# A two-block transformer layer in split float32: weight and feed-forward tiles placed 8 to 96 bytes further on in SBUF

## The chip, the cores and the metric

One core of a Trainium2 chip runs the kernel. The metric is the device time of one execution, in microseconds (us); smaller is better. A row names engines as PE (TensorE matmuls), PEld (TensorE weight loads), DVE (VectorE), ACT (ScalarE), POOL (GpSimd) and SP (SyncE, which issues the transfers).

## The reference, cut to what matters

A hybrid layer (pooling mixer, top-k attention, short convolution, feed-forward) is followed by a second layer (feed-forward, forgetting attention and stick-breaking attention, feed-forward, gated embedding). The model width is 1024, there are 512 tokens (528 with 16 meta tokens in the first layer), everything is float32. The change concerns only where the operands of the large products lie. Most of them come from the projections and from three feed-forward blocks of this form:

```
gate, up = jnp.split(hn @ w_gate_up, 2, axis=-1)      # 1024 x 5632
return h + (jax.nn.silu(gate) * up) @ w_down          # 2816 x 1024
...
x = x + 0.5 * swiglu(rms_norm_2(x, ffn1_norm), ffn1_w_gate, ffn1_w_up, ffn1_w_down)
...
x = x + 0.5 * swiglu(rms_norm_2(x, ffn2_norm), ffn2_w_gate, ffn2_w_up, ffn2_w_down)
```

## The kernel before, in words

Activations lie transposed in SBUF: features over the 128 partitions, tokens along a row. Every product is made of three matmuls, since each float32 operand is split in a high part in a reduced format (`F32R`) and a low part that is the rest: weights high times activation high (L608), weights high times activation low (L609), weights low times activation high (L610). In `passes` the weights are the stationary operand (loaded by a weight load, PEld) and the activations the moving one, mostly 512 columns of 4 bytes.

The weights come in 174 chunks of up to 2048 columns for each partition. A chunk c goes through two slots, c % 2: SP loads it into `raw[:, c % 2]`, ACT writes its high part into `whi[:, c % 2]` (L1079), POOL the low part into `wlo[:, c % 2]` (L500), PE uses both. A chunk of a square product is 8 row blocks k of 256 columns, so that PE's weight tiles start every 512 bytes in a slot. `chunk` walks t (2 output tiles) and k (8), three matmuls each; `pair` and the down projection in `ffn` do the same with other operands. The moving operands are `xh`/`xl` (the normalized activations, rows of 576 elements of which columns 16 to 527 are used by most chunks and all 528, in two halves of 264, by a few), the mixer and attention tiles in an arena, and in the down projection of each feed-forward block `fh`/`fl`, 22 rows of 512 elements. `fh` is written by ACT (L1123) and `fl` by DVE (L1584) while the gate and up projections run; PE reads both only in the down projection.

Placement: tiles are allocated one behind the other, rounded to 32 bytes, and `lead` pads the arena so that its start leaves 128 when divided by 256. Adding up the sizes gives that both slots of `whi` and `wlo`, column 16 of every row of `xh` and `xl`, and every row of `fh`, `fl` and of the other moving tiles of L608 to L610 leave the same 128. So in the products with 512 columns all operands have one phase modulo 256 bytes. Exceptions are the two halves of 264 columns (192 and 224 bytes from the weights' phase), the 8-column weights of chunk `C_FL` (a step of 32 bytes with each k), and in the stick-breaking attention `sk21`, the moving tile of L977 for odd heads, which starts 64 bytes before that phase; for even heads `sk20` has the common phase. L977 is followed there by L978, a 128-column matmul.

Of the kernel before, what the change touches and what calls it, by code (L numbers as in the profile page):

```python
# [20 lines left out]
F32 = mybir.dt.float32  # L21
F32R = mybir.dt.float32r
ACT = mybir.ActivationFunctionType
ALU = mybir.AluOpType
AX = mybir.AxisListType

P = 128
D = 1024
DK = D // P
T = 512  # L30
# [5 lines left out]
CH = 2048  # L36
# [9 lines left out]
FK = D_FF // P  # L46
HEAD_DIM = 64
DOWN_K = (8, 8, 6)
NEG = -1.0e30
UNITS = 4  # L50
Z_TOP = 60.0
TAKEN = -3.0e38
# [35 lines left out]
def lin(value, per=0, i=None):  # L88

    return value if i is None else i * per + value  # L90


def one(t, n):

    return t[:, n, :] if isinstance(n, int) else t[:, bass.ds(n, 1), :].rearrange("p o t -> p (o t)")
# [7 lines left out]
def build(nc, I, out):  # L103
    with ExitStack() as ctx:
        def sb(name, shape, dt=F32):
            return ctx.enter_context(nc.sbuf_tensor(name, shape, dt))
# [9 lines left out]
        eps = sb("eps", [P, 1])  # L116
        m8 = sb("m8", [P, 8])
        raw = sb("raw", [P, 2, CH])
        whi = sb("whi", [P, 2, CH], F32R)
        wlo = sb("wlo", [P, 2, CH], F32R)  # L120
        rs = sb("rs", [P, TM])
        rt = sb("rt", [P, TM])
        sq = sb("sq", [P, TM])
# [26 lines left out]
        def at(name, off, shape, dt=F32):  # L150
            n = 1
            for s in shape[1:]:
                n *= s
            assert off + n <= arena_cols, name
            return nc.alloc_sbuf_tensor_at(name, shape, dt, offset=start + 4 * off)


        fh = at("fh", 0, [P, FK, T], F32R)
        fl = at("fl", FK * T, [P, FK, T], F32R)
        tmp = at("tmp", 2 * FK * T, [P, 4, T])  # L160
        sq2, ssum2 = tmp[:, 0, :], tmp[:, 1, :]

        cT = at("cT", 0, [P, TM])
# [52 lines left out]
        rtq = at("rtq", 22528, [P, 4, T])  # L216
        pu = at("pu", 22528, [P, UNITS, T])
        sel = at("sel", 24576, [P, HEADS, P])
# [46 lines left out]
        silu_done, h_done, h_hi, h_split = sem("silu_done"), sem("h_done"), sem("h_hi"), sem("h_split")  # L265
# [215 lines left out]
        def _(pool):  # L481
# [6 lines left out]
            pool.affine_select(out=ident[:], in_=ident[:], compare_op=ALU.not_equal, fill=1.0, base=0, **tri).then_inc(consts, 1)  # L488
            pool.affine_select(out=causal[:], in_=causal[:], compare_op=ALU.is_ge, fill=NEG, base=0, **tri).then_inc(consts, 1)
            pool.affine_select(out=strict[:], in_=strict[:], compare_op=ALU.is_ge, fill=NEG, base=-1, **tri).then_inc(consts, 1)  # L490
            for z, o in enumerate((0, HEAD_DIM)):
# [113 lines left out]
        def _(pe):  # L605
# [74 lines left out]
            def ffn(f, S, X):  # L680
                c = C_F[f]

                chunk(c, xh, xl, X=X, between=lambda: norm_sums(S, c))
                chunk(c + 1, xh, xl)
                with pe.Fori(0, FK // 2 - 1) as i:
                    for j in range(2):
                        chunk(c + 2 + j, xh, xl, 2, i)
                c = C_D[f]
                with pe.Fori(0, 2) as i:
                    for j in range(2):  # L690
                        for r, kn in enumerate(DOWN_K):
                            cr, k0 = c + 3 * j + r, sum(DOWN_K[:r])
                            pe.wait_ge(w_lo, lin(cr + 1, 6, i))
                            if j == 0:
                                pe.wait_ge(h_split, FK * f + k0 + kn)
                            for t in range(2):
                                if r == 0:

                                    pe.wait_ge(acc_free, lin(2 * (c - 2 + j) + t + 1, 4 * j + 2 * t + 6, i))
                                for k in range(kn):  # L700
                                    o = CW * k + P * t
                                    mm = passes(ps[:, bank(c + j, t), :], cr % 2, lambda wt: wt[:, cr % 2, o:o + P],
                                                fh[:, k0 + k, :], fl[:, k0 + k, :], r == 0 and k == 0, r == 2 and k == kn - 1)
                                mm.then_inc(tile_done, 1)


# [350 lines left out]
            for n in range(DK):  # L1057
                if n >= 4:
                    pe.wait_ge(acc_free, 2 * C_PP + n - 3)
                for k in range(2):  # L1060
                    o = D * k + P * n
# [6 lines left out]
        def _(act):  # L1068
# [46 lines left out]
            def ffn(f, S, gain):  # L1115
                c = C_F[f]

                def up(c, n, per=0, i=None):
                    high(c + 2, per, i)
                    act.wait_ge(acc_free, lin(2 * c + 1, 2 * per, i))  # L1120
                    act.activation(tmp[:, 1, :], tmp[:, 0, :], ACT.Silu).then_inc(silu_done, 1)  # L1121
                    act.wait_ge(h_done, lin(FK * f + n + 1, per, i))
                    act.activation(one(fh, lin(n, per, i)), tmp[:, 3, :], ACT.Copy).then_inc(h_hi, 1)  # L1123

                root(S)
                if f == 1:
                    act.wait_ge(ms2_done, 1)
                    act.activation(rt[:, META:TM], ssum2, ACT.Sqrt, bias=eps[:], scale=1.0 / D).then_inc(rt2_done, 1)
                act.preload_act_table_set("silu_and_others")
                with act.Fori(0, FK // 2) as i:  # L1130
                    for j in range(2):
                        up(c + j, j, 2, i)
                d = C_D[f]
                with act.Fori(0, 2) as i:
                    for j in range(2):
                        high(d + 3 * j + 2, 6, i)
                        high(d + 3 * j + 3, 6, i)
                        act.wait_ge(acc_free, lin(2 * d + 6 * j + 3, 12, i))
                        feed(S + 1, 2 * j, gain, 4, i)
                        act.wait_ge(acc_free, lin(2 * d + 6 * j + 6, 12, i))  # L1140
                        feed(S + 1, 2 * j + 1, gain, 4, i)
                        high(d + 3 * j + 4, 6, i)
# [122 lines left out]
            for slot in range(4 * 2 * DK):  # L1265
                n = DSA_STEPS.get(slot)
# [225 lines left out]
        def _(dve):  # L1492
# [75 lines left out]
            def ffn(f, S, factor, gain):  # L1568
                c = C_F[f]
                if f == 1:  # L1570
                    closing_root()
                else:
                    root(S)
                with dve.Fori(0, FK // 2) as i:
                    for j in range(2):
                        n = FK * f + j
                        scaled(tmp[:, 0, :], c + j, 0, 2, i)
                        scaled(tmp[:, 2, :], c + j, 1, 2, i)
                        dve.wait_ge(silu_done, lin(n + 1, 2, i))
                        dve.wait_ge(acc_free, lin(2 * (c + j) + 2, 4, i))  # L1580
                        dve.tensor_tensor(tmp[:, 3, :], tmp[:, 1, :], tmp[:, 2, :], ALU.mult).then_inc(h_done, 1)  # L1581
                        dve.wait_ge(h_hi, lin(n + 1, 2, i))
                        nn = lin(j, 2, i)
                        dve.tensor_tensor(one(fl, nn), tmp[:, 3, :], one(fh, nn).bitcast(F32), ALU.subtract).then_inc(h_split, 1)  # L1584
                        dve.wait_ge(h_split, lin(n + 1, 2, i))
                d = C_D[f]
                if f == 1:
                    for n in range(DK):
                        x = hT[:, n, META:TM]
                        stt(x, x, vec[:, V_FIN + n:V_FIN + n + 1], ssum[:, META:TM], ALU.mult, ALU.mult).then_inc(xn_done, 1)  # L1590
                    dve.wait_ge(xn_done, DK)
                clear(S + 1)
                if S + 1 == 2:
                    dve.memset(ssum2, 0.0).then_inc(ssum2_done, 1)
                with dve.Fori(0, 2) as i:
                    for j in range(2):
                        for t in range(2):
                            n = 2 * j + t
                            done(d + 3 * j + 2, t, 6, i)
                            update(n, bank(d + j, t), factor, 3, 4, i)  # L1600
                            dve.wait_ge(acc_free, lin(2 * d + 6 * j + 3 * t + 3, 12, i))
                            feed(S + 1, n, gain, 4, i)
# [40 lines left out]
            for g in range(4):  # L1643
                r = slice(D_IDX * g, D_IDX * g + D_IDX)
# [25 lines left out]
            def search():  # L1670
                for q in range(QB):
# [4 lines left out]

                    link(stt(diag, causal[:], -TAKEN / -NEG, diag, ALU.mult, ALU.add))
                    for _ in range(TOP_K // 8):
# [3 lines left out]

                    link(dve.tensor_scalar(s, s, TAKEN, NEG, ALU.not_equal, ALU.mult))
                    link(dve.tensor_tensor(diag, diag, causal[:], ALU.add))
# [127 lines left out]
            for slot in range(4 * 2 * DK):  # L1812
                if slot % DK == DK - 1:
                    scaled(gb[:, slot // DK, :], C_GB + slot // (2 * DK), slot // DK % 2)
                n = DSA_STEPS.get(slot)
# [20 lines left out]
            with dve.Fori(0, 2) as i:  # L1836
                for n in range(4):
                    c, t = C_WB + n // 2, n % 2
# [66 lines left out]
            for z in range(2):  # L1905
                r = far(z).start + 32
# [119 lines left out]
            with dve.Fori(0, 2) as i:  # L2026
                for q in range(2):
                    c = C_MX + q
                    for t in range(2):
                        n = 2 * q + t  # L2030
# [62 lines left out]
```

## Time and profile before

| what | value |
|---|---|
| median of 3 runs | 2062.28 us (2061.86 to 2062.54) |
| profiled execution | 2061.71 us |
| its span in the trace | 2059.9 us |
| TensorE matmuls, busy | 2038.7 us, 9561 instructions |
| TensorE weight loads, busy | 1670.4 us |
| GpSimd / VectorE / ScalarE busy | 1009.8 / 883.7 / 734.4 us |
| DMA, mean | 91 GB/s |

A matmul's busy time overlaps that of its neighbours (a 512-column one is shown with 0.39 us, but a new one starts every 0.23 us), so the step from one start to the next is what counts, and it is read from a timeline. The granted clock of TensorE is 1.00, 2.4 GHz, in the stretches shown.

### The profile page before, as it was taken

The numbers are of one execution on the slowest core, as the hardware profiler recorded it, in microseconds if no ns is written. First come the engines' busy times: TensorE is split into PE (matmuls) and PEld (weight loads), VectorE is DVE, ScalarE is ACT, GpSimd is POOL, SyncE is SP. The second block draws the span as 40 slices with busy tenths as digits, with TensorE's granted clock in tenths as the row PEclk, the third lists the DMA queues.
The fourth block names the chain that finished last, engine by engine and source line by source line (L and its number), as shares of the span: only waits on it lengthen the run. The fifth ranks groups of instructions, "written<-read, shape, count | busy, mean of one in ns | idle before, by whom it ended". The sixth has DMA issues, their size and how long they took to land.

```text
span 2059.9 us, 26668 instructions
## 1 busy us (share of the span) xinstructions
PE 2038.7 (99%) x9561; PEld 1670.4 (81%) x9561; DVE 883.7 (43%) x1394; ACT 734.4 (36%) x1006; POOL 1009.8 (49%) x779
## 2 busy tenths in 40 slices
PE   8999999999999999999999999999999999999999
PEld 6798887678888888888888887888778888888887
DVE  6778645534333322153334113577744533332124
ACT  6413224433322223232222224566644422222232
POOL 5345442135555554455555444665544555554543
PEclk9999999999999999999999999999999999999999
DMA  4232322022333332333333232332222333333232
GB/s 159 66 103 83 103 89 74 21 79 85 102 102 100 85 96 93 99 100 102 98 86 97 92 98 82 107 99 72 70 64 82 102 102 98 86 101 97 92 107 82
DMA packets 254153, 188.21 MB, mean 91 GB/s; under 512 B 7552, under 2 KB 249728, under 8 KB 254080
## 3 DMA queue, kind: packets, MB, share of 16 engines
q1 hardware_dynamic: 253392, 186.93, 30.3%
q8 instruction: 44, 0.72, 0.1%
q10 hardware_dynamic: 688, 0.31, 0.1%
q14 instruction: 29, 0.24, 0.0%
HBM read 180.93 MB, written 2.10 MB: 89 GB/s over the span
## 4 chain that ended last, share of the span: by engine, by line
PE 95%; DVE 3%; issue 1%; ACT 1%; DMA 0%; SPq 0%; DVEq 0%; ACTq 0%
PE ps L608 29%; PE ps L610 29%; PE ps L609 29%; DVE sc L1502 1%; PE ps L988 1%; PE ps L829 1%; PE ps L895 1%; PE ps L814 1%; PE ps L897 1%; PE ps L896 1%; PE ps L960 0%; DVE ssum L1630 0%; PE ps L828 0%; PE ps L822 0%; PE ps L1002 0%
## 5 line engine op out<-in xcount | busy, mean ns | idle before, releaser
L500 POOL TENSOR_TENSOR wlo<-raw,whi 128x512 fp32r<-128x512 f32 (+1 forms) x640 | 870.6, 1391 | 923.3 <-ACT whi L1079 916.4
L608 PE MATMUL ps<-xh,whi 128*128 128x512 f32 (+2 forms) x1912 | 735.5, 385 | 9.3 <-DVE xl L1502 7.3
L610 PE MATMUL ps<-xh,wlo 128*128 128x512 f32 (+2 forms) x1912 | 722.1, 378 | 0.0
L609 PE MATMUL ps<-xl,whi 128*128 128x512 f32 (+2 forms) x1912 | 721.8, 378 | 0.0
L1079 ACT ACTIVATE whi<-raw 128x2048 fp32r<-128x2048 f32 (+1 forms) x159 | 297.6, 1871 | 797.8 <-PE ps L610 794.7
L608 PEld LDWEIGHTS ps<-xh,whi 128*128 128x128 f32 (+1 forms) x1912 | 357.9, 187 | 91.7 <-issue 23.9
L610 PEld LDWEIGHTS ps<-xh,wlo 128*128 128x128 f32 (+1 forms) x1912 | 357.7, 187 | 67.9
L609 PEld LDWEIGHTS ps<-xl,whi 128*128 128x128 f32 (+1 forms) x1912 | 358.3, 187 | 64.6 <-issue 2.5
L1556 DVE TENSOR_TENSOR tmp<-ps,rs 128x512 f32<-128x512 f32 x148 | 102.1, 691 | 325.9 <-PE ps L610 308.6
L608 PE MATMUL ps<-fh,whi 128*128 128x512 f32 x528 | 205.4, 389 | 0.0
L609 PE MATMUL ps<-fl,whi 128*128 128x512 f32 x528 | 205.4, 389 | 0.0
L610 PE MATMUL ps<-fh,wlo 128*128 128x512 f32 x528 | 205.4, 389 | 0.0
L1502 DVE SCALAR_TENSOR_TENSOR hT<-ps,hT 128x512 f32 x40 | 27.6, 691 | 271.0 <-PE ps L610 270.0
L1581 DVE TENSOR_TENSOR tmp<-tmp 128x512 f32<-128x512 f32 x66 | 90.2, 1367 | 114.3 <-ACT tmp L1121 114.2
L609 PEld LDWEIGHTS ps<-fl,whi 128*128 128x128 f32 x528 | 99.1, 188 | 20.6
L610 PEld LDWEIGHTS ps<-fh,wlo 128*128 128x128 f32 x528 | 99.1, 188 | 20.6
L608 PEld LDWEIGHTS ps<-fh,whi 128*128 128x128 f32 x528 | 99.1, 188 | 20.5
L555 POOL TENSOR_TENSOR wlo<-raw,whi 128x384 fp32r<-128x384 f32 (+1 forms) x78 | 77.1, 1016 | 42.8 <-ACT whi L1374 41.8
L1084 ACT ACTIVATE xh<-hT,vec (+1 forms) x48 | 34.4, 725 | 125.3 <-DVE hT L1502 125.3
L1123 ACT ACTIVATE fh<-tmp 128x512 f32 x66 | 41.8, 633 | 101.2 <-DVE tmp L1581 101.2
L1584 DVE TENSOR_TENSOR fl<-tmp,fh 128x512 f32 x66 | 51.0, 773 | 61.2 <-ACT fh L1123 61.2
L1502 DVE SCALAR_TENSOR_TENSOR xl<-hT,vec,xh (+1 forms) x48 | 47.0, 989 | 55.1 <-ACT xh L1084 55.1
(293 smaller groups left out, 2195.7 us busy)
## 6 DMA issues: line engine op xcount, KB each, us to landing
raw<-in_w_in SPq DMA_DIRECT2D x90, 512.0 KB, 4.6
raw<-in_w_gate_up SPq DMA_DIRECT2D x44, 512.0 KB, 4.7
raw<-in_ffn_w_gate SPq DMA_DIRECT2D x44, 512.0 KB, 3.9
raw<-in_ffn_w_up SPq DMA_DIRECT2D x44, 512.0 KB, 5.1
raw<-in_ffn_w_down SPq DMA_DIRECT2D x32, 512.0 KB, 4.0
raw<-in_w_down SPq DMA_DIRECT2D x16, 512.0 KB, 3.9
raw<-in_ffn_w_down SPq DMA_DIRECT2D x16, 384.0 KB, 3.5
raw<-in_w_b SPq DMA_DIRECT2D x8, 512.0 KB, 4.0
```

What stands on the lines that cost most here:

```text
L500: ins = pool.tensor_tensor(wlo[:, c % 2, cs], raw[:, c % 2, cs], whi[:, c % 2, cs].bitcast(F32), ALU.subtract)
L555: ins = pool.tensor_tensor(wlo[:, c % 2, cs], raw[:, c % 2, cs], whi[:, c % 2, cs].bitcast(F32), ALU.subtract)
L608: pe.matmul(o, w_of(whi), xhi, start=first, stop=False)
L609: pe.matmul(o, w_of(whi), xlo, start=False, stop=False)
L610: return pe.matmul(o, w_of(wlo), xhi, start=False, stop=last)
L1079: act.activation(whi[:, c % 2, 0:n], raw[:, c % 2, 0:n], ACT.Copy).then_inc(w_hi, 1)
L1084: act.activation(one(xh, nn)[:, lo:TM], one(hT, nn)[:, lo:TM], ACT.Copy, scale=col(vec, lin(gain + n, per, i))).then_inc(xh_done, 1)
L1123: act.activation(one(fh, lin(n, per, i)), tmp[:, 3, :], ACT.Copy).then_inc(h_hi, 1)
L1502: return dve.scalar_tensor_tensor(o, a, s, b, op0, op1)
L1556: dve.tensor_tensor(o, ps[0:o.shape[0], bank(c, t), :], rsx[0:o.shape[0]], ALU.mult).then_inc(acc_free, 1)
L1581: dve.tensor_tensor(tmp[:, 3, :], tmp[:, 1, :], tmp[:, 2, :], ALU.mult).then_inc(h_done, 1)
L1584: dve.tensor_tensor(one(fl, nn), tmp[:, 3, :], one(fh, nn).bitcast(F32), ALU.subtract).then_inc(h_split, 1)
```

## The change

The rows of `whi` and `wlo` get 4 more elements for each slot, so that the second slot of each starts 16 bytes later in phase than the first. A filler tile `aside` of 56 elements keeps `wlo` at the common phase. What is allocated behind `wlo` (`rs` to `fbias`, among them `ident`, `identr`, `strictr` and the place that `sk11` and `sk21` take) moves by 288 bytes, 32 in phase; `lead` puts the arena back on its phase. `fh` and `fl` become three views each in two wider tiles, which start 2, 8 and 24 elements (8, 32 and 96 bytes) into them, one for each feed-forward block; `tmp` moves by 512 bytes. No instruction, wait or transfer is added or removed, and shapes and order stay.

```diff
+F_AT = (2, 8, 24)
...
-        whi = sb("whi", [P, 2, CH], F32R)
-        wlo = sb("wlo", [P, 2, CH], F32R)
+        whi = sb("whi", [P, 2, CH + 4], F32R)
+        aside = sb("aside", [P, 56])
+        wlo = sb("wlo", [P, 2, CH + 4], F32R)
...
-        fh = at("fh", 0, [P, FK, T], F32R)
-        fl = at("fl", FK * T, [P, FK, T], F32R)
-        tmp = at("tmp", 2 * FK * T, [P, 4, T])
+        fhw = at("fhw", 0, [P, FK * T + 32], F32R)
+        flw = at("flw", FK * T + 32, [P, FK * T + 64], F32R)
+        fh = [fhw[:, o:o + FK * T].rearrange("p (k t) -> p k t", k=FK) for o in F_AT]
+        fl = [flw[:, 32 + o:32 + o + FK * T].rearrange("p (k t) -> p k t", k=FK) for o in F_AT]
+        tmp = at("tmp", 2 * FK * T + 128, [P, 4, T])
...
-                                                fh[:, k0 + k, :], fl[:, k0 + k, :], r == 0 and k == 0, r == 2 and k == kn - 1)
+                                                fh[f][:, k0 + k, :], fl[f][:, k0 + k, :], r == 0 and k == 0, r == 2 and k == kn - 1)
...
-                    act.activation(one(fh, lin(n, per, i)), tmp[:, 3, :], ACT.Copy).then_inc(h_hi, 1)
+                    act.activation(one(fh[f], lin(n, per, i)), tmp[:, 3, :], ACT.Copy).then_inc(h_hi, 1)
...
-                        dve.tensor_tensor(one(fl, nn), tmp[:, 3, :], one(fh, nn).bitcast(F32), ALU.subtract).then_inc(h_split, 1)
+                        dve.tensor_tensor(one(fl[f], nn), tmp[:, 3, :], one(fh[f], nn).bitcast(F32), ALU.subtract).then_inc(h_split, 1)
```

## Rows read from the trace of the kernel before

**Rows 1.** The page: span, busy time by engine, and the chain by engine

```profile
span 2059.9 us, 26668 instructions
...
PE 2038.7 (99%) x9561; PEld 1670.4 (81%) x9561; DVE 883.7 (43%) x1394; ACT 734.4 (36%) x1006; POOL 1009.8 (49%) x779
...
PE 95%; DVE 3%; issue 1%; ACT 1%; DMA 0%; SPq 0%; DVEq 0%; ACTq 0%
```

**Rows 2.** PE's groups by form: count, busy us, mean ns, idle before

```profile
L608 PE MATMUL ps<-xh,whi 128*128 128x512 f32 x1680 | 667.1, 397 | 1.4 <-POOL wlo L500 1.4
...
L608 PE MATMUL ps<-fh,whi 128*128 128x512 f32 x528 | 205.4, 389 | 0.0
L609 PE MATMUL ps<-fl,whi 128*128 128x512 f32 x528 | 205.4, 389 | 0.0
```

**Rows 3.** Timeline of PE, 560 to 604: first and last of 196 matmuls

```profile
559.71 0.39 PE L609 MATMUL ps<-xl,whi 128*128 128x512 f32 x1
...
603.91 0.39 PE L609 MATMUL ps<-xl,whi 128*128 128x512 f32 x1
```

**Rows 4.** Busy time of each engine in one gate-and-up stretch, with the clock

```profile
540.00:740.00 200.00, 200.00 (x884) 165.62 (x883) 66.18 (x75) 55.84 (x55) 111.05 (x76) 1.00 0.34 94
```

**Rows 5.** Instructions of the tile fh: ns min/median/max, starts of first and last

```profile
L608 PE MATMUL ps<-fh,whi x528: 389/389/396, 754.6 to 1998.7; 128*128 128x512 f32 x176
L610 PE MATMUL ps<-fh,wlo x528: 389/389/396, 755.1 to 1999.2; 128*128 128x512 f32 x176
L1123 ACT ACTIVATE fh<-tmp x66: 631/633/634, 530.3 to 1883.9; 128x512 f32 x66
L1584 DVE TENSOR_TENSOR fl<-tmp,fh x66: 743/775/786, 531.1 to 1884.7; 128x512 f32 x66
```

**Rows 6.** L977, then L978, of an even head (1441 us) and an odd one (1455 us)

```profile
L977 PE MATMUL ps<-sk,sq x1: 389/389/389, 1441.5 to 1441.5; 128*128 128x512 f32 x1
...
L978 PE MATMUL ps<-strictr,identr x1: 224/224/224, 1441.7 to 1441.7; 128*128 128x128 f32 x1
...
L977 PE MATMUL ps<-sk,sq x1: 394/394/394, 1455.2 to 1455.2; 128*128 128x512 f32 x1
...
L978 PE MATMUL ps<-strictr,identr x1: 220/220/220, 1455.4 to 1455.4; 128*128 128x128 f32 x1
```

**Rows 7.** Timeline of PE with 8-column weights: first and last of 19 matmuls

```profile
1285.98 0.39 PE L608 MATMUL ps<-xh,whi 128*8 128x512 f32 x1
...
1290.14 0.39 PE L608 MATMUL ps<-xh,whi 128*8 128x512 f32 x1
```

**Rows 8.** Timeline of PE with 264 columns: first and last of 195 matmuls

```profile
119.78 0.28 PE L609 MATMUL ps<-xl,whi 128*128 128x264 f32 x1
...
143.38 0.29 PE L608 MATMUL ps<-xh,whi 128*128 128x264 f32 x1
```

**Rows 9.** Timeline of PE behind an interruption: first, tenth and nineteenth matmul

```profile
881.74 0.40 PE L609 MATMUL ps<-xl,whi 128*128 128x512 f32 x1
...
883.83 0.39 PE L609 MATMUL ps<-xl,whi 128*128 128x512 f32 x1
...
885.87 0.39 PE L609 MATMUL ps<-xl,whi 128*128 128x512 f32 x1
```

**Rows 10.** The page: the casts of the weights, ACT and POOL, by line

```profile
L500 POOL TENSOR_TENSOR wlo<-raw,whi 128x512 fp32r<-128x512 f32 (+1 forms) x640 | 870.6, 1391 | 923.3 <-ACT whi L1079 916.4
...
L1079 ACT ACTIVATE whi<-raw 128x2048 fp32r<-128x2048 f32 (+1 forms) x159 | 297.6, 1871 | 797.8 <-PE ps L610 794.7
```

## The prediction

> **What bounds the kernel now.** I read the page first. PE is busy 2038.7 of 2059.9 us, and the chain that ended last lies on PE for 95% [rows 1]. So the time is the number of matmuls times the step from one start to the next, and a change of placement can act only through that step, unless it makes another engine late. Second, the groups of PE by form: the 512-column matmuls of L608 to L610 are 3 x 1680 = 5040 with `xh`/`xl` and 3 x 528 = 1584 with `fh`/`fl` [rows 2]; by the loops of `chunk` and `pair`, another 1008 read mixer and attention tiles (three times 64 for each of three pairs of tiles, 32 for each of four, 16 x 3 for `pTh`). That is 7632, with next to no idle time before them. Third, the timeline, for the step. Between 559.71 and 603.91 us lie 195 steps: 44.20 / 195 = 226.67 ns [rows 3]. 512 columns at 2.4 GHz (the granted clock around it is 1.00 [rows 4]) are 213.33 ns, so each step holds 13.3 ns that are not columns. The same step holds for `fh`: its matmuls are shown with 389 ns at the minimum and in the median alike [rows 5], as those of the steady stretch are. One ns on all 7632 steps would be 7.6 us, 0.37%. The reader should see in these rows how little a placement has to cost to be measured, and that nothing else stands between PE and the end.
>
> **What the trace says of phase.** All operands of that steady stream have one phase modulo 256 bytes before the change. Three places of the trace have another.
>
> First, L977 in the stick-breaking attention. Same shape, same stationary tile in kind, but the moving tile of odd heads lies 64 bytes off. The even head at 1441 us shows 389 ns, the odd one at 1455 us 394 ns; all four even and all four odd heads with 512 columns repeat it. The L978 behind it gives something back: 224 against 220 ns [rows 6]. So a phase does act on PE, by +5 ns alone and by +1 ns net of the follower.
>
> Second, the 8-column weights, which move on by 32 bytes with each k while the moving tile stays in phase. From 1285.98 to 1290.14 us are 18 steps, six triples, 4.16 / 6 = 693.3 ns for each [rows 7]; three steady steps are 680.0. So each advance of the weights' phase goes with 13.3 ns.
>
> Third, the 264-column halves, 64 and 32 bytes before the weights' phase, alternating with each triple. From 119.78 to 143.38 us are 194 steps of 121.6 ns [rows 8], with 110.0 ns of columns: 11.6 ns above the columns, no more than the steady 13.3. This speaks against a loss.
>
> Then there is what happens behind an interruption, with all operands in phase: nine steps take 2.09 us, the next nine 2.04 [rows 9]. PE needs about ten matmuls to fall into its steady step and until then pays 0.05 us / 9, about 5 ns each. I take this as the price of a stream that does not fall into step.
>
> The Trainium skill ("SBUF — State Buffer", Who interferes with whom) says that TensorE has two independent SBUF read ports and waits for nobody. By that rule the sum would be nothing for every edit; the 389 against 394 ns just named does not agree with it, so I keep it as a rival and not as the base.
>
> **The change, part by part.** No instruction is added, so every term is a difference of step.
>
> `fh`/`fl` of the second and third block, 32 and 96 bytes off: 2 x 528 = 1056 matmuls. The nearest row is L977's, off by 64: I take its 5 ns, 5.3 us. Below, its net 1 ns gives 1.1 us; a gain of 5 ns, which no row excludes, gives -5.3 us.
>
> `fh`/`fl` of the first block, 8 bytes off: 528 matmuls. It is nearest to phase 0, so I take 0; above, 5 ns gives 2.6 us, and below, the same as a gain.
>
> Slot 1 with a steady moving tile: half of 7632, 3816 matmuls whose weights lie 16 bytes off. Within a chunk the offset does not change, and no row has a small constant offset. Nearest is phase 0 again: I take 0. Above: if the stream does not fall into step, 5 ns x 3816 = 19.1 us. Below: a gain of 5 ns would be -19.1 us.
>
> The change of phase between chunks: 174 chunks alternate the slots, 173 borders. Nearest is the advance of the 8-column weights, 13.3 ns each: 2.3 us. Below 0; above a whole time of settling, 0.05 us x 173 = 8.7 us.
>
> The 264-column and 256-column products of slot 1, and the transposes and L976 to L978, whose tiles behind `wlo` move by 32 bytes: each some 500 matmuls. By the 264-column row such offsets cost nothing: 0, with 5 ns x 1000 = 5 us as the bound to either side.
>
> The writers. POOL casts 512 columns in 1391 ns, four pieces for a chunk, and ACT one chunk in 1871 ns [rows 10]: 5.6 and 1.9 us, against 48 x 226.67 ns = 10.9 us that PE takes for it. ACT writes a row of `fh` in 633 ns, DVE one of `fl` in 775 ns [rows 5]. In the gate-and-up stretch POOL is busy 111 of 200 us, DVE 66, ACT 56 [rows 4]. This slack hides writes at an uneven start: they would have to take nearly twice the time before PE waits. If that cover were gone, each of 22 x 3 rows 10% slower would be 66 x 0.14 = 9 us. I take 0. The transfers land in `raw`, which does not move.
>
> The sum: 5.3 + 0 + 0 + 2.3 + 0 = +7.6 us. Against the profiled execution's own 2061.71 us (its span of 2059.9 and 1.8 around it) this is 2069.3; the median of the runs is 0.6 higher, so 2069.9 us, +0.37%.
>
> **The rivals.** *Nothing changes: 2062.3 us.* The step is the same for streams in every stage, and the 264-column stretch has two offsets with no loss. If a constant offset only shifts where PE settles, the step stays at 226.67 and the borders cost too little to see. Against it stands the odd head's 394 ns. This is also what the skill's rule on the ports would give.
>
> *Out of step.* If an offset between weights and moving tile keeps the stream from settling, all 3816 slot-1 matmuls pay 5 ns, and so do the 792 of `fh`/`fl` in slot 0: 4608 x 5 = 23.0 us, 2085.3 us. For it: settling was only ever seen with all operands in phase. Against: the 8-column weights keep a regular pattern, 13.3 ns and not 15.
>
> *Faster.* Equal phases may be what makes the 13.3 ns: two streams, weights and columns, that touch the same part of SBUF at the same time. Shifts of 8 to 96 bytes part them. A step lower by the 5 ns that one phase cost in the odd heads gives 1584 x 5 = 7.9 us on `fh`/`fl`, 2054.4 us; if slot 1 gains as well, 23 us, 2039.3. It decides from a net gain of 4.1 us, 2.6 ns on each `fh`/`fl` matmul. For it: 264 columns off phase carry 11.6 ns above their columns against 13.3. Against it: the one clean pair of rows has the loss on the side of the offset, and the 8-column weights, which hardly read SBUF, step no faster.
>
> **How the numbers follow.** About 0.2% (4.1 us) is what a measurement of this kernel can tell from no change. I give the forecast 0.32 and "out of step" 0.14, so slower 0.46; no change 0.33; faster 0.21, half of it below 2054. The range goes from 2054 to 2084 us: it leaves out 0.10 below and 0.09 above. Taken alone, the slower side lies between 2066.4 and 2087.
>
> **What the profile after would show.** Right: the minimum of the `fh` and `fl` matmuls stays 389 ns in the first block and stands at 394 or more in the second and third (or the step in their stretches at 231 to 233 ns), the steady `xh` stretch stays at 226.67 ns in both slots, with a few longer steps behind each border. Wrong: `fh` at 389 throughout and the same step (no change), steps near 232 in every second chunk (out of step), or durations below 389 and steps below 226 (faster). If PE's idle time before L608 grows, a writer became the bound, which none of the terms holds.

## The result, and the profile after

The changed kernel takes 2071.23 us (median of 4, 2071.09 to 2072.47) against 2062.07 us for the kernel before, a ratio of 1.0046 with a 95% interval of 1.0033 to 1.0060. It is slower by 9.2 us; 2069.9 had been forecast, +7.6. The profiled execution took 2071.20 us, its span is 2069.4.

The page of the changed kernel, first the span and busy times, then the chain. It answers to [rows 1]: PE has 9.7 us more of busy time for the same 9561 matmuls, and no other engine came into the chain.

```profile
span 2069.4 us, 26734 instructions
...
PE 2048.4 (99%) x9561; PEld 1671.5 (81%) x9561; DVE 876.8 (42%) x1394; ACT 735.2 (36%) x1006; POOL 1013.0 (49%) x779
...
PE 96%; DVE 2%; ACT 0%; issue 0%; DMA 0%; SPq 0%; DVEq 0%; ACTq 0%
```

The groups of PE by form, against [rows 2]. The `xh` group stands at 397 ns as before; the feed-forward tiles, now called `fhw` and `flw`, went from 389 to 393 and 394 ns. The idle time before the feed-forward tiles is still 0.0.

```profile
L612 PE MATMUL ps<-xh,whi 128*128 128x512 f32 x1680 | 667.5, 397 | 1.5 <-POOL wlo L504 1.5
...
L613 PE MATMUL ps<-flw,whi 128*128 128x512 f32 x528 | 208.0, 394 | 0.0
L612 PE MATMUL ps<-fhw,whi 128*128 128x512 f32 x528 | 207.8, 394 | 0.0
L614 PE MATMUL ps<-fhw,wlo 128*128 128x512 f32 x528 | 207.4, 393 | 0.0
```

The timeline of PE in the steady gate-and-up stretch, against [rows 3]: first and last of 196 matmuls, over chunks of both slots. 44.20 / 195 = 226.67 ns, as before. So a weight tile 16 bytes off, alternating with one that is not, and the border between them cost nothing here.

```profile
559.66 0.39 PE L614 MATMUL ps<-xh,wlo 128*128 128x512 f32 x1
...
603.86 0.39 PE L614 MATMUL ps<-xh,wlo 128*128 128x512 f32 x1
```

The down projections, in the same view: for each block the second and the last matmul of two chunks that follow each other. 46 steps lie between the two rows of each pair. The slots are those of the chunk numbers: the first and the second block begin with chunks 60 and 94, in slot 0, the third with chunk 157, in slot 1. The chunks shown are 63 and 64, 97 and 98, 160 and 161, so the slots are 1 and 0 in the first two blocks and 0 and 1 in the third.

```profile
785.98 0.40 PE L613 MATMUL ps<-flw,whi 128*128 128x512 f32 x1
...
796.67 0.40 PE L614 MATMUL ps<-fhw,wlo 128*128 128x512 f32 x1
...
797.14 0.39 PE L613 MATMUL ps<-flw,whi 128*128 128x512 f32 x1
...
807.84 0.39 PE L614 MATMUL ps<-fhw,wlo 128*128 128x512 f32 x1
...
1149.64 0.39 PE L613 MATMUL ps<-flw,whi 128*128 128x512 f32 x1
...
1160.07 0.40 PE L614 MATMUL ps<-fhw,wlo 128*128 128x512 f32 x1
...
1160.54 0.40 PE L613 MATMUL ps<-flw,whi 128*128 128x512 f32 x1
...
1171.27 0.39 PE L614 MATMUL ps<-fhw,wlo 128*128 128x512 f32 x1
...
1916.66 0.40 PE L613 MATMUL ps<-flw,whi 128*128 128x512 f32 x1
...
1927.41 0.40 PE L614 MATMUL ps<-fhw,wlo 128*128 128x512 f32 x1
...
1927.88 0.39 PE L613 MATMUL ps<-flw,whi 128*128 128x512 f32 x1
...
1938.46 0.39 PE L614 MATMUL ps<-fhw,wlo 128*128 128x512 f32 x1
```

The reader divides each difference by 46: 232.4 and 232.6 ns in the first block (8 bytes off), 226.7 and 233.3 in the second (32 off), slot 1 named first in both, and in the third (96 off) 230.0 in slot 1 and 233.7 in slot 0. Above 226.67 ns, halved over the slots and times 528 matmuls, that is 3.1 + 1.8 + 2.7 = 7.6 us. The other 1.9 us of the 9.5 by which the span grew lie outside the down projections. Laid beside the trace of before, matmul by matmul, they come in a few stretches of slot 1 chunks, 27 to 37, 185 to 192, 1278 to 1289, 1579 to 1592, 1602 to 1614, 2008 to 2021 and 2054 to 2065 us; there the step is 233 ns where it was 226.67. Most of them begin where the stream is interrupted, by a wait or by matmuls of another kind. The first experiment shows the same.

The writers, in the view by tile, against [rows 5]: ACT takes 634 ns for a row against 633. DVE even takes less, 693 against 775 ns, which brings nothing, since PE does not wait for it.

```profile
L1127 ACT ACTIVATE fhw<-tmp x66: 632/634/637, 530.8 to 1890.1; 128x512 f32 x66
L1588 DVE TENSOR_TENSOR flw<-tmp,fhw x66: 691/693/696, 531.6 to 1891.0; 128x512 f32 x66
```

### The profile page after: what moved, and what is told of

Same layout as the page of the kernel before. It is cut to its first block, busy times and chain, and to the rows that moved or that the text cites. A ratio compares the mean times of both kernels' runs of the same rounds, so it can differ in the third digit from the quotient of the medians.

```text
span 2069.4 us, 26734 instructions
## 1 busy us (share of the span) xinstructions
PE 2048.4 (99%) x9561; PEld 1671.5 (81%) x9561; DVE 876.8 (42%) x1394; ACT 735.2 (36%) x1006; POOL 1013.0 (49%) x779
## 4 chain that ended last, share of the span: by engine, by line
PE 96%; DVE 2%; ACT 0%; issue 0%; DMA 0%; SPq 0%; DVEq 0%; ACTq 0%
PE ps L612 29%; PE ps L613 29%; PE ps L614 29%; DVE sc L1506 1%; PE ps L992 1%; PE ps L833 1%; PE ps L818 1%; PE ps L899 1%; PE ps L900 1%; PE ps L901 1%; PE ps L964 0%; DVE ssum L1634 0%; PE ps L826 0%; PE ps L832 0%; PE ps L1006 0%
## 5 line engine op out<-in xcount | busy, mean ns | idle before, releaser
L613 PE MATMUL ps<-flw,whi 128*128 128x512 f32 x528 | 208.0, 394 | 0.0
L612 PE MATMUL ps<-fhw,whi 128*128 128x512 f32 x528 | 207.8, 394 | 0.0
L614 PE MATMUL ps<-fhw,wlo 128*128 128x512 f32 x528 | 207.4, 393 | 0.0
L613 PEld LDWEIGHTS ps<-flw,whi 128*128 128x128 f32 x528 | 99.5, 188 | 22.8
L614 PEld LDWEIGHTS ps<-fhw,wlo 128*128 128x128 f32 x528 | 99.4, 188 | 22.8
L612 PEld LDWEIGHTS ps<-fhw,whi 128*128 128x128 f32 x528 | 99.1, 188 | 23.0
L1127 ACT ACTIVATE fhw<-tmp 128x512 f32 x66 | 41.9, 634 | 102.1 <-DVE tmp L1585 102.1
L1588 DVE TENSOR_TENSOR flw<-tmp,fhw 128x512 f32 x66 | 45.7, 693 | 68.5 <-ACT fhw L1127 68.5
```

The lines of the kernel that those rows point to most:

```text
L612: pe.matmul(o, w_of(whi), xhi, start=first, stop=False)
L613: pe.matmul(o, w_of(whi), xlo, start=False, stop=False)
L614: return pe.matmul(o, w_of(wlo), xhi, start=False, stop=last)
L1127: act.activation(one(fh[f], lin(n, per, i)), tmp[:, 3, :], ACT.Copy).then_inc(h_hi, 1)
L1588: dve.tensor_tensor(one(fl[f], nn), tmp[:, 3, :], one(fh[f], nn).bitcast(F32), ALU.subtract).then_inc(h_split, 1)
```

## The experiments

All use one template of the kernel before. Both weight tiles and both feed-forward tiles become views with an adjustable start, the tiles get 256 bytes of room each, so that everything else keeps its phase modulo 256, and five constants set the starts in elements of 4 bytes:

```diff
+W_AT, LO_AT, SLOT1 = 0, 0, 4              # start of whi, of wlo, further offset of slot 1
+FH_AT, FL_AT = (0, 0, 0), (0, 0, 0)       # start of fh and fl, for each block
...
-        whi = sb("whi", [P, 2, CH], F32R)
-        wlo = sb("wlo", [P, 2, CH], F32R)
+        whw = sb("whw", [P, 2 * CH + 64], F32R)
+        wlw = sb("wlw", [P, 2 * CH + 64], F32R)
+        whi, wlo = (w[:, o:o + 2 * (CH + SLOT1)].rearrange("p (s n) -> p s n", s=2) for w, o in ((whw, W_AT), (wlw, LO_AT)))
```

**The slot alone.** The constants as shown.

> Only the second slot of both weight tiles is moved by 16 bytes; the feed-forward tiles and all other tiles keep the common phase. Theory A (the step depends on the difference of phase between moving tile and weights, and a difference of 16 bytes is free): every steady 512-column step stays at 226.67 ns in both slots, 2062.1 us within 0.1%. Rival (the borders between slots cost a settling time each, up to 8.7 us): 2064 to 2071 us, with longer steps behind each border.

Measured: 2063.4 us (11 runs) against 2061.85, ratio 1.0007 with an interval of 0.9998 to 1.0016. The steady step with `xh` is (603.93 - 559.73) / 195 = 226.67 ns, over both slots:

```profile
559.73 0.39 PE L613 MATMUL ps<-xh,whw 128*128 128x512 f32 x1
...
603.93 0.39 PE L613 MATMUL ps<-xh,whw 128*128 128x512 f32 x1
```

The down projections step at 226.67 ns too. So in steady stretches neither the 16 bytes nor a border costs anything, as theory A said. What is left is 1.5 us by the medians, not clear of zero by the interval, and 1.2 us in the spans. The trace shows where it arises: in four slot 1 chunks, at 185, 1273, 1575 and 1597 us. The twelfth and the last matmul of the last of them, the first chunk with `m2h`/`m2l`, lie 36 steps apart:

```profile
1599.50 0.39 PE L615 MATMUL ps<-m2h,wlw 128*128 128x512 f32 x1
...
1607.90 0.40 PE L615 MATMUL ps<-m2h,wlw 128*128 128x512 f32 x1
```

That is 8.40 / 36 = 233.3 ns up to the end of the chunk. In the kernel before, the same 36 steps take 8.16 us (1598.46 to 1606.62), 226.7 ns, and two chunks on, in the same slot with the same tiles, the step here is 226.7 ns again (1619.48 to 1629.68 us, 45 steps). So the same pair of phases, weights 16 bytes on and moving tile at the common phase, runs in two ways in one trace, at 226.67 ns nearly everywhere and at 233.3 ns in these chunks. Three of them stand behind an interruption of the stream, that at 1575 us does not; and behind two other interruptions in slot 1, at 27 and 2007 us, the step is 226.7. So an interruption often goes with the slower way, and what decides is open. A chunk with equal phases is back at 226.67 ns after about ten matmuls [rows 9].

**The feed-forward tiles alone.**

```diff
+W_AT, LO_AT, SLOT1 = 0, 0, 0
+FH_AT, FL_AT = (2, 8, 24), (2, 8, 24)
```

> Only the feed-forward tiles are moved, by 8, 32 and 96 bytes; both weight slots keep the common phase. Theory A: the steps of the changed kernel's slot 0 hold in both slots (232.6, 233.2 and 230.1 ns), 528 x (5.9 + 6.5 + 3.4) ns = +8.4 us, 2070.5 us. Rival B (the loss comes from the alternation of two weight phases under an uneven moving tile, not from the tile's own offset): the steps fall back to 226.67 ns and the time to 2062 us.

Measured: 2072.28 us, ratio 1.0050 (1.0037 to 1.0064). The timeline, one chunk of each block (46 steps each; slot 0 in the first two, slot 1 in the third): 232.6, 233.3 and 233.5 ns, and within 0.3 ns the same in the other slot.

```profile
796.50 0.39 PE L614 MATMUL ps<-flw,whw 128*128 128x512 f32 x1
...
807.20 0.39 PE L615 MATMUL ps<-fhw,wlw 128*128 128x512 f32 x1
...
1160.59 0.40 PE L614 MATMUL ps<-flw,whw 128*128 128x512 f32 x1
...
1171.32 0.40 PE L615 MATMUL ps<-fhw,wlw 128*128 128x512 f32 x1
...
1928.42 0.40 PE L614 MATMUL ps<-flw,whw 128*128 128x512 f32 x1
...
1939.16 0.40 PE L615 MATMUL ps<-fhw,wlw 128*128 128x512 f32 x1
```

Rival B fell: the tiles' own offset is enough. The third block was expected at 230.1 ns and shows 233.5. That expectation had the slots of the third block the wrong way round: 230.1 ns is the changed kernel's slot 1 there, and its slot 0, with the pair of phases of this run, stands at 233.7. In the down projections this part alone costs 10.2 us and both parts together 7.6, since the 16 bytes in slot 1 make the second block free there and the third block cheaper.

**Both parts, in the template.**

```diff
+W_AT, LO_AT, SLOT1 = 0, 0, 4
+FH_AT, FL_AT = (2, 8, 24), (2, 8, 24)
```

> Both parts of the change together, but with the tiles behind the weights and the arena at the phases of before modulo 512 bytes. Theory F (the same pair of phases can run in two patterns, and which one depends on what came before, here on the alternation of the slots): the steps by block and slot are those of the changed kernel, third block slot 0 at 230.0 ns and not 233.3, 2071 us. Rival (the difference between the changed kernel and the feed-forward part alone comes from the arena's shift by 256 bytes): third block slot 0 at 233.3 ns, 2073 us.

Measured: 2071.93 us, ratio 1.0049 (1.0029 to 1.0068), and the steps of the changed kernel in every block and slot. In the third block slot 0 steps at (1928.80 - 1918.05) / 46 = 233.7 ns, slot 1 at (1939.85 - 1929.26) / 46 = 230.2:

```profile
1918.05 0.40 PE L614 MATMUL ps<-flw,whw 128*128 128x512 f32 x1
...
1928.80 0.40 PE L615 MATMUL ps<-fhw,wlw 128*128 128x512 f32 x1
...
1929.26 0.39 PE L614 MATMUL ps<-flw,whw 128*128 128x512 f32 x1
...
1939.85 0.39 PE L615 MATMUL ps<-fhw,wlw 128*128 128x512 f32 x1
```

Placement in slot 0 is the same in this run and the one before it, and its steps agree, 233.7 here and 233.3 there; only slot 1, whose weights moved, differs. So what theory F expected of this block did not come: slot 0 is not at 230.0. There was nothing for it, or for its rival, to explain; both rest on the swapped slots. That one pair of phases can run in two ways is shown all the same, by the slot alone above and by the runs with 16 and 32 bytes below.

**Other offsets of the moving tile.** Three kernels, one run each, weights at the common phase:

```diff
+FH_AT, FL_AT = (1, 3, 4), (1, 3, 4)
...
+FH_AT, FL_AT = (16, 32, 48), (16, 32, 48)
...
+FH_AT, FL_AT = (12, 20, 28), (12, 20, 28)
```

> Feed-forward tiles at 4, 12 and 16 bytes, weights at the common phase. Theory A with lines of 16 bytes: 226.67 ns in the third block, about 232 ns in the first and second. Rival (any offset of the moving tile costs, and the free 16 bytes seen in slot 1 with xh are a property of the weights' side): about 232 ns in all three.

> Feed-forward tiles at 64, 128 and 192 bytes, weights at the common phase. If what counts is the difference modulo 64 bytes: 226.67 ns in all three blocks. If it is modulo 128: 226.67 ns in the second block, and the same larger step (233 ns, as the odd heads of L977 show) in the first and third. If it is modulo 256 or more: the second block is slow as well.

> Feed-forward tiles at 48, 80 and 112 bytes, weights at the common phase. Theory E: all three out of phase and multiples of 16, so 228.9 to 233.3 ns, 2068 to 2073 us. A step below 226.67 ns in any block would say that equal phases are not the best placement.

Measured: 2072.11, 2069.75 and 2069.76 us. Theory A with lines of 16 bytes fell: 16 bytes cost 5 ns. So did its rival, which expected about 232 ns in all three blocks of the first kernel: 4, 12 and 16 bytes give 238.0, 228.9 and 231.6. At 48, 80 and 112 bytes the steps are 233.3, 231.1 and 231.2, none below 226.67. Neither 64 nor 128 bytes is a period: (1158.27 - 1147.54) / 46 = 233.3 ns at 128, though 64 has one of the two smallest losses, (795.45 - 784.92) / 46 = 228.9.

```profile
784.92 0.39 PE L614 MATMUL ps<-flw,whw 128*128 128x512 f32 x1
...
795.45 0.39 PE L615 MATMUL ps<-fhw,wlw 128*128 128x512 f32 x1
...
1147.54 0.39 PE L614 MATMUL ps<-flw,whw 128*128 128x512 f32 x1
...
1158.27 0.39 PE L615 MATMUL ps<-fhw,wlw 128*128 128x512 f32 x1
```

**The weights moved as a whole.** Three kernels, one run each: is it the difference that counts, or the moving tile's own start?

```diff
+W_AT, LO_AT, SLOT1 = 2, 2, 0
+FH_AT, FL_AT = (2, 0, 4), (2, 0, 4)
...
+W_AT, LO_AT, SLOT1 = 4, 4, 0
+FH_AT, FL_AT = (4, 0, 8), (4, 0, 8)
...
+W_AT, LO_AT, SLOT1 = 8, 8, 0
+FH_AT, FL_AT = (8, 0, 16), (8, 0, 16)
```

> Both slots of both weight tiles 8 bytes on; feed-forward tiles at 8, 0 and 16 bytes; xh stays. Theory D (the difference between moving tile and weights counts): the first block, again in one phase with its weights, steps at 226.67 ns; the second, the third and all 5040 matmuls with xh, each 8 bytes apart, step near 232.6 ns, so about +28 us on xh and +6 us on two blocks, 2096 us. Theory C (the moving tile's own start counts, the weights' does not): xh and the second block stay at 226.67 ns, the first at 232.6 and the third at 231.7, 2068 us.

> Both slots of both weight tiles 16 bytes on; feed-forward tiles at 16, 0 and 32 bytes; xh stays. Theory E (steps are 226.67 ns when weights and moving tile have one phase modulo 256 that is a multiple of 16, and a moving tile 16 bytes behind its weights is free too): first block, second block and all of xh 226.67 ns, third block (16 ahead) 231.7 ns; 2064 to 2066 us. Rival (the free 16 bytes behind were free only because every second chunk had equal phases): xh and second block near 231 ns, +22 us or more.

> Both slots of both weight tiles 32 bytes on; feed-forward tiles at 32, 0 and 64 bytes; xh stays. Theory D: first block 226.67 ns, xh and second block (32 bytes behind) about 233 ns, +32 us on xh, third block (32 ahead) 233.3 ns; near 2100 us. Theory C: xh and second block 226.67 ns, first 233.3, third 228.9; 2067 us.

Measured: 2087.51, 2099.69 and 2103.93 us, far larger losses than before, since now all of `xh` is out of phase. Theory C (only the moving tile counts) is gone: with weights 32 on, `xh` steps at (603.95 - 559.62) / 190 = 233.3 ns and the first block, 32 bytes on with its weights, at (810.89 - 800.47) / 46 = 226.5.

```profile
559.62 0.40 PE L613 MATMUL ps<-xh,whw 128*128 128x512 f32 x1
...
603.95 0.40 PE L614 MATMUL ps<-xl,whw 128*128 128x512 f32 x1
...
800.47 0.39 PE L614 MATMUL ps<-flw,whw 128*128 128x512 f32 x1
...
810.89 0.39 PE L615 MATMUL ps<-fhw,wlw 128*128 128x512 f32 x1
```

Theory D (only the difference counts) is gone as well. With both tiles 8 bytes on, in one phase, the first block steps at (802.23 - 791.50) / 46 = 233.3 ns; with both 16 on at 230.0. And theory E fell on two points: with weights 16 on, `xh` steps at (603.91 - 559.81) / 189 = 233.3 ns, where the slot alone had left the same pair of phases at 226.67; and the third block, 16 ahead of its weights, is free, (1956.81 - 1946.38) / 46 = 226.7, where 16 ahead of weights at 0 cost 5 ns.

```profile
559.81 0.39 PE L614 MATMUL ps<-xl,whw 128*128 128x512 f32 x1
...
603.91 0.39 PE L614 MATMUL ps<-xl,whw 128*128 128x512 f32 x1
...
1946.38 0.39 PE L614 MATMUL ps<-flw,whw 128*128 128x512 f32 x1
...
1956.81 0.39 PE L615 MATMUL ps<-fhw,wlw 128*128 128x512 f32 x1
```

The rival named in that expectation is right that `xh` 16 bytes behind its weights is not free when both slots are moved, though the step is 233.3 ns and not 231. Its reason, that every second chunk must have equal phases, is too narrow, as the last run shows.

**High and low tiles apart, and the low weights alone.** Two kernels, one run each.

```diff
+FH_AT, FL_AT = (0, 0, 32), (4, 32, 0)
...
+W_AT, LO_AT, SLOT1 = 0, 8, 0
+FH_AT, FL_AT = (0, 8, 32), (0, 8, 32)
```

> Weights at the common phase; in the first block fh at 0 and fl at 16 bytes, in the second fh at 0 and fl at 128, in the third fh at 128 and fl at 0. If each moving tile pays for its own offset, the first two blocks have one matmul of three slow (228.3 and 228.9 ns on average) and the third two of three (231.1 ns). If what counts is the change of phase from one moving tile to the next, all three have two changes in three matmuls and are slow alike, whichever of the two tiles is moved.

> Only wlo is 32 bytes on, whi stays; feed-forward tiles at 0, 32 and 128 bytes. Theory D: one weight load of three is out of phase with xh and with the first block, which step at about 229 ns on average (+11 us on xh); second block worse. Theory C: xh and first block stay at 226.67 ns, second 233.3, third 233.3.

Measured: 2066.94 and 2106.66 us. In the first, the steps are 232.0, 229.0 and 228.9 ns: neither a sum over single tiles (the first block was to be 228.3, the third 231.1) nor the same for all three. In the second, one weight load of three out of phase is as bad as all three: `xh` and all blocks step at 233.3 ns. So the tiles do not each pay for themselves; the step belongs to the whole sequence of three.

**Does a stream in step stay in step?** Slot 1 by 32 bytes in place of 16, one run.

```diff
+W_AT, LO_AT, SLOT1 = 0, 0, 8
+FH_AT, FL_AT = (0, 8, 4), (0, 8, 4)
```

> Only the second slot of both weight tiles is moved, by 32 bytes; feed-forward tiles at 0, 32 and 16 bytes. Theory F in its general form (a stream that is in step when it comes to an uneven chunk stays in step): xh and the first block stay at 226.67 ns in both slots, though both slots at 32 bytes gave 233.3 ns; about 2067 us with the two other blocks. Rival (only the 16-byte offset has two patterns): xh steps at 226.67 ns in slot 0 and near 233 ns in slot 1, +16 us, 2083 us or more, and each slot 0 chunk begins with some longer steps.

Measured: 2084.08 us. It does not at 32 bytes: the first block steps at 233.3 ns in slot 1 (792.32 to 803.05 us) and at 226.7 in slot 0, and `xh` does the same. The second block, 32 bytes on, has it the other way round.

```profile
792.32 0.39 PE L614 MATMUL ps<-flw,whw 128*128 128x512 f32 x1
...
803.05 0.40 PE L615 MATMUL ps<-fhw,wlw 128*128 128x512 f32 x1
```

The third block of this kernel, at 16 bytes, says more on 16 bytes behind. In slot 1 (weights at 32) its first chunk steps at (1910.53 - 1899.79) / 46 = 233.5 ns and each of the five later ones at 226.7, as (1951.82 - 1941.39) / 46 here:

```profile
1899.79 0.40 PE L614 MATMUL ps<-flw,whw 128*128 128x512 f32 x1
...
1910.53 0.40 PE L615 MATMUL ps<-fhw,wlw 128*128 128x512 f32 x1
...
1941.39 0.39 PE L614 MATMUL ps<-flw,whw 128*128 128x512 f32 x1
...
1951.82 0.39 PE L615 MATMUL ps<-fhw,wlw 128*128 128x512 f32 x1
```

The slot 0 chunks between them are 16 bytes ahead of their weights and step at 231.7 ns. So no neighbour of the later chunks has equal phases, and 16 behind is free there all the same. Steps as far apart as 226.7 and 233.3 ns for one pair of phases were seen only for a moving tile 16 bytes behind its weights; what decides between them was not settled.

The steps of all runs but those with high and low tiles apart, each from a timeline as above, in ns. "Moving" and "weights" are bytes past the common phase:

| weights | moving: step |
|---|---|
| 0, both slots | 0: 226.7; 4: 238.0; 8: 232.6; 12: 228.9; 16: 231.6; 32: 233.3; 48: 233.3; 64: 228.9; 80: 231.1; 96: 233.4; 112: 231.2; 128: 233.3; 192: 233.3 |
| 8, both slots | 0: 230.6; 8: 233.3; 16: 231.1 |
| 16, both slots | 0: 233.3; 16: 230.0; 32: 226.7 |
| 32, both slots | 0: 233.3; 32: 226.7; 64: 233.4 |
| 16 in slot 1, 0 in slot 0 | slot 1, 0: 226.7 (233.3 in a few chunks); 8: 232.4; 32: 226.7; 96: 230.1. Slot 0, 0: 226.7; 8: 232.6; 32: 233.3; 96: 233.6 |
| 32 in slot 1, 0 in slot 0 | slot 1, 0: 233.3; 32: 226.7; 16: 226.7 (first chunk 233.5). Slot 0, 0: 226.7; 32: 233.3; 16: 231.7 |

## Why the prediction was right, and where it was not

The direction and nearly the size are right, and so is what bounds the kernel: no engine but PE changed the time, the writers' slack held, and the step carried the whole loss. That the sum came as near as 7.6 to 9.2 us is partly luck, since one term was missing and another stood for something else. Point by point:

The term for `fh`/`fl` of the second and third block, 5.3 us from L977's 5 ns, measured 1.8 + 2.7 = 4.5 us. But 5 ns is an average over things that differ: three of the four block-and-slot pairs lost 3 to 7 ns and one lost nothing. The offset of L977 itself, 64 bytes before the phase, is 192 in the table, and in a steady stream it costs 6.6 ns.

The term for the first block was mis-sized. I took 0 since 8 bytes are near to phase 0, and it measured 3.1 us, 5.8 ns on each matmul. The prediction's own sign of being right, the first block unchanged, did not come. Nearness in bytes is no guide: 4 bytes off is the worst offset found, 238.0 ns.

Slot 1 with a steady moving tile was taken at 0 and measured 0 in the steady stretches. This was right by luck of the arrangement: with both slots 16 bytes on, the same pair of phases costs 233.3 - 226.7 = 6.6 ns, and that kernel took 38 us longer. My "out of step" rival was the mechanism of that kernel. In the changed kernel it acts in a few slot 1 chunks only, and its price of 5 ns was too low.

The 173 borders were taken at 2.3 us. In the steady stretches they cost nothing. Outside the down projections the span grew by 1.9 us, and with the slot alone by 1.2 (2061.1 against 2059.9). Nearly all of it lies in the few slot 1 chunks that run at 233 ns; that the size is about that of the term is a coincidence.

The "nothing changes" rival went with a rule of the Trainium skill ("SBUF — State Buffer", Who interferes with whom): TensorE has two independent read ports and waits for nobody. The traces do not agree with what the rival made of it. The step depends on both starts together: moving `wlo` alone by 32 bytes takes `xh` from 226.7 to 233.3 ns, and a block whose moving tiles go 32 bytes on together with both weight tiles is back at 226.5. This says that the two streams are not independent; whether they meet in SBUF or within TensorE no run here tells.

The 16-byte lines that the same page of the Trainium skill states (Specifications (TRN2)) do not explain the table: 16, 32, 48 and 128 bytes off are whole lines and cost 5 to 6.6 ns.

The "faster" rival fell in every stretch that was measured: of the pairs of the table none steps below 226.7 ns. What the 13.3 ns above the columns are is open, and so are the rule behind the table and the mechanism. That the starts cause the loss is shown; why they do is not. Equal phases at a multiple of 32 bytes gave the lowest step in both cases tried (0 and 32), equal phases at 8 and 16 did not.

## What to carry to other kernels

Where matmuls in split float32 follow each other without a gap, the start addresses of the stationary and the moving tile are worth up to 11 ns in 227. Put both at one phase modulo 256 bytes (a shift by 256 was free: the changed kernel's arena has one, and its other tiles kept their steps) and on a multiple of 32, all rows included, and check every kind of chunk in a timeline, since a mean over a stage hides it. Do not test an offset in one of two alternating buffers and carry the answer to both: the 16 bytes that were nearly free in one slot went with 38 us in two. And before a step is put down to a slot, work the slot out from the chunk's number; where a block begins with an odd chunk, the order is turned.

## What the runs showed of the hardware that was not expected

The steps are periodic and repeat to the ns. With `wlo` off, the step goes 233, 239, 228 ns again and again; slot 1 in the third block of the changed kernel goes 226, 229, 236, 229. The means (226.7, 228.9, 230.0, 231.1, 233.3) recur in stretches with different offsets.

With the weights 8 bytes on, POOL's cast is faster, 1219 against 1429 ns on average for the same 512 columns (by form; [rows 10] mixes two forms), and DVE's subtraction into `fl` is slower, 1595 against 773 ns on average. The trace shows what goes with the second: in 65 of the 66 subtractions a cast of POOL starts 5 to 58 ns before the subtraction, which then ends about 550 ns after the cast; in the kernel before, the cast starts 157 to 200 ns after the subtraction. The one subtraction with no cast starting beside it took 693 ns. So it is the order of the two that changed with the faster cast, and no effect of the start on DVE is shown. From the kernel with the weights 8 bytes on, POOL's group, one cast and the subtraction beside it:

```profile
L505 POOL TENSOR_TENSOR wlw<-raw,whw 128x512 fp32r<-128x512 f32 x588 | 698.9, 1219 | 1025.2 <-ACT whw L1084 1018.1 <-ACT whw L1379 7.1
...
532.72 1.09 POOL L505 TENSOR_TENSOR wlw<-raw,whw 128x512 fp32r<-128x512 f32 x1
...
532.75 1.61 DVE L1589 TENSOR_TENSOR flw<-tmp,fhw 128x512 f32 x1 [0.95 <-ACT fhw L1128]
```

In the kernel before, the subtraction at 531.12 us takes 0.78 us and the cast at 531.31 us 1.74. Here both are hidden; in a kernel bound by these engines they would not be. Why the cast is faster was not tested, and the order as the cause of the slower subtraction is read from the trace, not tested by a run.
